# Differential attention on one core: head norm and exponentials later in each engine's order, weights scaled in one pass, mask by matmul, output projection in two parts

## The reference

```python
kv = rmsnorm(h, kv_norm_g) @ kv_w          # k1, k2: 64 wide, v: 128 wide, for each of 8 heads
qq = rmsnorm(h, b_norm_g) @ b_w_q          # q1, q2: 64 wide
k1, k2, q1, q2 = (apply_partial_rope(rmsnorm(.., g), cos, sin))   # norm over 64, rotation
...
def probs(qb, kk):
    s = einsum('bhqd,bhkd->bhqk', qb, kk) * scale
    return softmax(where(causal, s, -inf), axis=-1)
w = probs(q1b, k1f) - lam * probs(q2b, k2f)     # a block of 128 queries at a time
o = einsum('bhqk,bhkd->bhqd', w, v)
o = rmsnorm(o, b_subln_g) * (1.0 - lam_init)    # norm over a head's 128
h = h + merge_heads(o) @ b_w_o
h = h + squared_relu_mlp(h, ...)
```

## Time and profile before

| what | value |
|---|---|
| median of 3 runs | 3060.82 us (3059.88 to 3062.23) |
| profiled execution, own time | 3060.37 us |
| its span | 3058.6 us |
| TensorE matmul busy | 2711.6 us (89%) |
| DVE busy | 1170.4 us (38%) |
| ACT busy | 1036.7 us (34%) |
| GpSimd busy | 878.5 us (29%) |
| differential attention and its projection | about 2221 to 2682 us of the span |

### The profile page before, as it was taken

The page is one execution under the profiler, slowest core; times in us unless marked ns, Lnnn a source line. Parts: engine busy times, 40 slices in busy tenths (PEclk is TensorE's granted clock), DMA queues, the critical chain, the costliest instruction groups (busy, mean ns, idle before and its releaser), DMA issues.

```text
span 3058.6 us, 42262 instructions
## 1 busy us (share of the span) xinstructions
PE 2711.6 (89%) x16806; PEld 2200.1 (72%) x16806; DVE 1170.4 (38%) x2247; ACT 1036.7 (34%) x2154; POOL 878.5 (29%) x612
## 2 busy tenths in 40 slices
PE   4999898999989888888888789999987787799999
PEld 3887687787865555556777579999976665577777
DVE  4654556432241112112255751422555555212112
ACT  3434444522232112113234444233244544332331
POOL 0001454322320223100322126555410000355653
PEclk8989999999989999999899889999998887799999
DMA  3322011233327999993211012332311110123332
GB/s 105 84 57 55 15 35 35 77 97 89 101 96 295 426 426 426 426 425 141 77 45 51 23 49 83 97 90 86 88 52 39 42 28 8 56 83 97 97 92 67
DMA packets 320134, 364.16 MB, mean 119 GB/s; under 512 B 14128, under 2 KB 293680, under 8 KB 295360
## 3 DMA queue, kind: packets, MB, share of 16 engines
q1 hardware_dynamic: 319936, 361.42, 34.0%
HBM read 359.29 MB, written 2.10 MB: 118 GB/s over the span
## 4 chain that ended last, share of the span: by engine, by line
PE 67%; DVE 11%; DMA 8%; ACT 7%; POOL 4%; issue 4%; DVEq 0%; ACTq 0%; SPq 0%; POOLq 0%
DMA early<-in_w_up_e 7%; PE bank L1703 5%; PE bank L2160 5%; PE bank L443 5%; PE bank L445 5%; PE bank L444 5%; PE bank L2161 5%; PE bank L2162 5%; PE bank L2591 4%; PE bank L2592 4%; PE bank L2593 4%; POOL split L2133 2%; ACT split L2117 1%; PE bank L1001 1%; DVE split L2136 1%
## 5 line engine op out<-in xcount | busy, mean ns | idle before, releaser
L2133 POOL TENSOR_TENSOR split<-keep,split 128x1024 fp32r<-128x1024 f32 x152 | 369.6, 2436 | 357.7 <-ACT split L2113 357.7
L2160 PE MATMUL bank<-x_hi,split 128*128 128x264 f32 (+1 forms) x1280 | 401.5, 314 | 12.6 <-POOL split L2133 8.3
L2161 PE MATMUL bank<-x_lo,split 128*128 128x264 f32 (+1 forms) x1280 | 395.9, 309 | 0.0
L2162 PE MATMUL bank<-x_hi,split 128*128 128x264 f32 (+1 forms) x1280 | 394.8, 308 | 0.0
L1703 PE MATMUL bank<-early 128*64 128x256 f32 x2048 | 236.0, 385 | 48.3 <-DMA early<-in_w_up_e 19.8
L2160 PEld LDWEIGHTS bank<-x_hi,split 128*128 128x128 f32 x1280 | 245.0, 191 | 40.8 <-issue 26.2
L1703 PEld LDWEIGHTS bank<-early 128*64 128x64 f32 x2048 | 170.7, 138 | 126.7 <-issue 52.9
L2161 PEld LDWEIGHTS bank<-x_lo,split 128*128 128x128 f32 x1280 | 245.3, 192 | 10.2
L2162 PEld LDWEIGHTS bank<-x_hi,split 128*128 128x128 f32 x1280 | 244.3, 191 | 10.9
L2113 ACT ACTIVATE split<-keep 128x1024 fp32r<-128x1024 f32 x168 | 175.4, 1050 | 224.3 <-PE bank L2593 210.8
L443 PE MATMUL bank<-x_hi,w_split 128*128 128x512 f32 x416 | 169.8, 408 | 15.7 <-DVE w_split L431 15.7
(11 more groups left out here) (458 smaller groups left out, 6227.5 us busy)
## 6 DMA issues: line engine op xcount, KB each, us to landing
early<-in_w_gate_e SPq DMA_DIRECT2D x64, 1024.0 KB, 11.0
early<-in_w_up_e SPq DMA_DIRECT2D x64, 1024.0 KB, 11.2
early<-in_w_down_e SPq DMA_DIRECT2D x64, 1024.0 KB, 10.6
early<-in_w_in SPq DMA_DIRECT2D x66, 512.0 KB, 3.7
keep<-in_mlp_w_in SPq DMA_DIRECT2D x64, 512.0 KB, 3.9
keep<-in_mlp_w_out SPq DMA_DIRECT2D x64, 512.0 KB, 4.0
keep<-in_a_w_qkv SPq DMA_DIRECT2D x24, 512.0 KB, 3.6
early<-in_w_ssd_out SPq DMA_DIRECT2D x16, 512.0 KB, 4.0
```

The source lines that it names most:

```text
L2133: e.tensor_tensor(lo, x, whole(hi), ALU.subtract).then_inc(*u.free(sig_, "lo", n))
L2160: e.matmul(o, hi[:, k, :], XH2[:, k, n0:n1], start=k == 0, stop=False, skip_group_check=True)
L2161: e.matmul(o, hi[:, k, :], XL2[:, k, n0:n1], start=False, stop=False, skip_group_check=True)
L2162: m = e.matmul(o, lo[:, k, :], XH2[:, k, n0:n1], start=False, stop=k == 7, skip_group_check=True)
```

## The change

- **Weights with a gain.** A new helper `split_gain` on DVE multiplies the loaded tile by its gain in place, in one tensor_tensor; `split_hi` and `split_lo` then treat all tiles alike, with one instruction each. `split_gain` runs up to one tile ahead of the copy. In the attention `split_hi` and `split_lo` go one tile further ahead for j = 0 to 3.
- **Order inside a step.** The pieces of a step are now h3, h1, c2, c1, c0, lin, (first), (second), h0, h2, ce. `c0` ends with the maximum; the exponentials and the mixing are the new piece `ce`, behind the step's `lin`. The head norm is cut into h0 (square, lag 4), h1 (sum, lag 6), h2 (root, lag 6) and h3 (scaling and split, lag 7), and uses the head's own q and k buffers in place of a score buffer.
- **Projection step on DVE.** Before: low split, V, (sine, sum) of both halves, scaling, PSUM copy. After: V, sine of both halves, scaling, gain, sum of both halves, low split, PSUM copy. GpSimd's cosine product waits for the rotation matmul, not for DVE's sine.
- **Mask.** Two matmuls of an fp32r identity with an fp32r mask add it to the scores' last 128 columns in PSUM. ACT makes both operands in `normb_act`; TensorE waits for them at the start of the attention. The maximum is now written negated.
- **Scores of the last query block** are issued half by half, the two softmaxes in turn.
- **Output projection in two parts.** Its weights are now 8 tiles of 4 heads by 256 columns, split by ACT and DVE. For each of the 8 output tiles the first four heads (12 matmuls) are done in the attention's late steps (`first`) and added to the residual; `second` does heads 4 to 6 for four output tiles in steps 34 and 37; `outb_pe` does the rest.

```diff
-        plan += [(wbo, 0, 8, c, 128, None) for c in COLS8]
+        plan += [(wbo, k0, 4, 256 * c, 256, None) for k0 in (0, 4) for c in range(4)]
...
+        def split_gain(e, upto):
...
+                if gain is not None:
+                    e.wait_ge(*KW.of(n).landed())
+                    x = split_parts(n)[0]
+                    e.tensor_tensor(x, x, bc(gain[:, k0:k0 + nk], nc_), ALU.mult).then_inc(*S.dve.up("gain", n))
...
-                    for k in range(nk):
-                        e.scalar_tensor_tensor(out=lo[:, k, :], in0=x[:, k, :], scalar=gain[:, k0 + k:k0 + k + 1],
-                                               in1=whole(hi[:, k, :]), op0=ALU.mult, op1=ALU.subtract).then_inc(*u.free(sig_, "lo", n))
+                e.tensor_tensor(lo, x, whole(hi), ALU.subtract).then_inc(*u.free(sig_, "lo", n))
...
+            for y, x in ((IDENT2, C["ident"]), (NEG2, C["amask"][:, 128:256])):
+                e.activation(y, x, ACT.Copy).then_inc(*LM.act.up("mask"))
...
-        for step in range(37):
-            ATTB += [(f, step - lag) for f, lag in (("c4", 5), ("c3", 4), ("c2", 3), ("c1", 2), ("c0", 0)) if 0 <= step - lag < 32]
+        PARTS = (24, 25, 26, 28, 29, 30, 32, 33)
+        for step in range(39):
...
+            ATTB += units(("h3", 7), ("h1", 6), ("c2", 3), ("c1", 2), ("c0", 0))
             p, n = step // 8, step % 8
             if p < 3:
                 ATTB += [("lin", (p + 1, j)) for j in ([n] if n < 7 else [7, 8])]
+            if step in PARTS:
+                ATTB.append(("first", PARTS.index(step)))
+            if step in (34, 37):
+                ATTB.append(("second", range(4, 6) if step == 34 else range(6, 7)))
+            ATTB += units(("h0", 4), ("h2", 6), ("ce", 0))
...
         def attb_pe(e):
+            e.wait_ge(*LM.act.to("mask"))
...
+                    for a in range(2):
+                        e.matmul(XR.of("score", i, a, h).ap[:, kl - 128 - k0:kl - k0], IDENT2, NEG2, start=False, stop=True,
+                                 skip_group_check=True).then_inc(*DA2.pe.up("score", i, a, h))
...
-                    split_hi(e, attb_weights(p, j) + (2 if j < 4 else 3))
+                    split_hi(e, attb_weights(p, j) + 3)
...
-                    e.tensor_tensor(dg, dg, bmid(C["amask"][:, 128:256], 2), ALU.add).then_inc(*DA2.dve.up())
-                    e.wait_ge(*DA2.dve.now())
-                    e.tensor_reduce(out=v[:, 0:2], in_=xv[:, :, 0:kl], op=ALU.max, axis=AX.X).then_inc(*DA2.dve.up())
-                    e.wait_ge(*DA2.dve.now())
-                    e.tensor_scalar(v[:, 2:4], v[:, 0:2], -1.0, None, ALU.mult).then_inc(*DA2.dve.up("max", i))
+                    e.tensor_reduce(out=v[:, 2:4], in_=xv[:, :, 0:kl], op=ALU.max, axis=AX.X, negate=True).then_inc(*DA2.dve.up("max", i))
+                if what == "first":
+                    split_lo(e, AT_WBO + i // 2 + 3, True)
+                    b, r = BR.of("oa", "b", i), R[:, i, 16:T2]
+                    e.wait_ge(*OB_.pe.to("first", i))
+                    e.tensor_tensor(r, r, b.ap[:, :], ALU.add).then_inc(*b.free(OB_.dve, "first", i))
...
-                        e.wait_ge(*PD.dve.to("sin", i[0], i[1] - 2, h))
+                        e.wait_ge(*PD.pe.to("rot", i[0], i[1] - 2, h))
```

156 lines of the change are left out of this document (106 added, 50 removed).

## The result

| what | before | changed |
|---|---|---|
| median in the first comparison | 3060.62 us (3059.88 to 3062.23) | 3014.61 us (3010.11 to 3016.47) |
| profiled execution, its span | 3060.37, 3058.6 us | 3014.8, 3013.0 us |
| mean granted clock | 0.941 | 0.952 |

The ratio is 0.9846, 95% interval 0.9834 to 0.9857: the kernel is faster by 46 us (44 to 51 by the interval). The forecast was 2986 us (2945 to 3030), 74 us less than before. The direction and the wide range hold. The narrow range of the forecast itself, 2966 to 3006 us, is missed by 9 us: over a third of the forecast gain isn't there.

A forecast was written before the change was run, and what follows sets the result against it. The prediction saw no engine full: TensorE idled on waits for V's weight split and the head norm's square, and paid again in clock. 3060.4 + 9 (start) - 45 (passes) - 38 (tail) = 2986 us, own range 2966 to 3006, wide 2945 to 3030.

The forecast's parts named there:

- Tail: Last units alone plus output projection: 78 us instead of 116, -38 us (-28 to -44), with projection matmuls beside late units.
- Start: First nine projection steps: new waits for the mask and behind the roots, shorter V wait, clock loss; +9 us (2 to 14).
- Lookahead and V's wait: V's second weight tile split a step ahead: TensorE's wait 3 us or less in a pass, near 5 at the start.
- Single pass over the weights: One DVE product, ACT copy and DVE subtraction per tile: product 1.23 us; ACT relieved of about 7 us in a pass.
- A pass: Eight units with nine projection steps: 62 + 1.2 + 9.5 + 6 = 79 us instead of 94, -15 each, -45 for three.
- All 37.1 us of waiting go: Moved head norm: TensorE's waits for its square vanish, except for the last head.
- Work in a pass: TensorE's work at full clock: 62 us from busy time by clock, plus 1.2 us for mask matmuls.
- MLP 1: Last MLP, after the output projection: first tile split in time, its 363 us don't move.
- Lock: Rival, 8%: GpSimd's cosine products each hold up a DVE operation on the path, 18 us in all; 3004 us.
- DVE's loop: Rival, 16%: DVE's loop sets the pass, new waits full, pass 89 us, start +14, tail -30; 3028 us.
- TensorE stays fed: Rival, 15%: DVE runs ahead and no bank is late; pass 67 us, start +6, tail -42; 2945 us.
- Slower: Rival, 4%: DVE, PSUM copy and next linear close a loop in all eight steps, 13.5 us each; pass 108, total 3086 us.

The follow-up runs named there:

- tail_late: Changed kernel with the output projection's `first` and `second` matmuls issued behind all attention units instead of between the late ones; 3034.83 us, ratio 0.9909 to before.
- norm_old: Changed kernel with the head norm's square, sum and root together again ahead of the product with V, as before the change; 3024.52 us, ratio 0.9882.
- mask_late: Changed kernel with TensorE's wait for the mask's copies moved to the first unit's mask matmul; 3002.98 us, ratio 0.9807 to before.
- weights_first: Changed kernel with DVE's gain product and low-split subtraction at the beginning of its projection step; 2978.36 us, ratio 0.9728 to before.
- gain_old: Changed kernel with weights made by 8 or 4 scaled ACT copies and fused DVE operations again, new lookahead kept; 3007.96 us, ratio 0.9830.
- lookahead_old: weights_first with high and low weight parts split one tile less ahead for k, k, q, q, as before the change; 3011.44 us, ratio 0.9838.
- square_late: Changed kernel with ACT's square of a projection step one step later, behind the next unit's score copy; 2985.83 us, ratio 0.9746 to before.
- root_early: Changed kernel with the head norm's root on ACT right behind the unit's scores instead of at the step's end; 2996.54 us, ratio 0.9781.
- four_moves: Changed kernel with the moves of root_early, square_late, weights_first and mask_late all together; 2943.94 us, ratio 0.9615 to before.
- moves_gain_old: four_moves with weights made by 8 or 4 scaled ACT copies and fused DVE operations again; 2949.56 us, ratio 0.9641 to before.

## Why the prediction was right or wrong, point by point

- **Tail: right, the exact hit partly by luck.** 78 us (-38) forecast, 77.7 us (-38.3) measured on the marks of the earlier trace rows. The hand schedule came to 75 us and was 2.7 us short; the 3 us added for the clock weren't lost (it is 1.00), and the two errors cancel. By tail_late 17 us come from the matmuls beside the units, by norm_old 11 from the head norm; the wait of 6.6 us ahead of the projection is gone as well. The last 4 us have no run.
- **Start: right in its parts.** +6 us by the windows, forecast +9 (2 to 14). The wait for the mask is 5.42 us (5.7 forecast), the split behind the roots 4.63 us (4), V's wait 4.98 us (5.5). mask_late takes away the first, weights_first the other two. Too large was the clock: 5.4 + 4.6 - 5 leaves about 1 us for it, where the forecast had 4.
- **Lookahead and V's wait: right.** "3 us or less in a pass" is 2.7, 2.7 and 1.6 us.
- **Single pass over the weights: right that it costs little.** The product over a broadcast gain has a mean of 1218 ns, the estimate was 1.23 us. gain_old and lookahead_old (the latter on weights_first) confirm that the lookahead counted and not the number of instructions.
- **A pass: wrong, -6.5 us instead of -15 (-7.1 like against like); this is the failed step.** The term "62 + 1.2 + 9.5 + 6 = 79" measured 87.5 (86.9). Its idle time is (262.5 - 219.6)/3 = 14.3 us, not 9.5, and of another kind. The prediction laid out DVE's queue only. It had the square waiting for DVE's PSUM copy, and the exponentials behind it, but asked only whether the *linears* would wait for a bank. It didn't go down ACT's own queue to see what else stands behind the square and which bank that frees. The three waits of linears, 2.0, 3.1 and 1.4 us, hardly exist: TensorE had been held earlier, by 5.97 us (two passes) and 6.7 us (all three), and finds DVE done afterwards. The passes' waits are the 23.1 us of scores and 11.9 us of the product with V, 7.0 us for V's split and 0.7 us: together 42.7 of the 42.9 us of idle time. square_late takes away the cause and root_early one of its two effects.
- **"All 37.1 us of waiting go": right in the letter only.** The sum no longer waits; but h2 now frees the sum's bank at the end of ACT's step, and the product with V waits for that. norm_old shows a move worth nothing within the passes. The prediction named this case ("only swaps one wait for another") inside a rival that it gave another cause.
- **Work in a pass: 3 us too small.** 62 us came from busy time by granted clock. At nearly full clock, in four_moves, the same product is 205.13 x 0.97 / 3 = 66.3 us, where the forecast had 63.2. Three things make up these 3.1 us. The later marks put 14 more matmuls into the passes, 0.6 us for each pass. The two mask matmuls of a unit take 0.28 us and not 0.14:

```profile
2554.68 0.44 PE L2824 MATMUL bank<-mask 128*128 128x128 f32 x2
2554.96 0.45 PE L2759 MATMUL bank<-b_hi,split 128*128 128x512 f32 x1
```

  That is 2.2 us in a pass instead of 1.2; the forecast took 0.07 us out of its bounds of 0.06 to 0.14, and 0.14 was right. The other 1.5 us are the product itself: a stretch's mean clock also counts the idle time, in which it was partly low (before, from 2500.80 to 2504.70 us, TensorE does nothing and the granted clock is 0.50), so the product falls short where there are waits. The start shows the same: 50.75 x 0.89 = 45 us before, 47.74 x 1.00 = 48 us in four_moves, and only 0.5 us of that are the first unit's scores. By these terms the pass's miss of 8.8 us is 4.8 us of idle time, 3.1 of work and 0.9 of clock.
- **MLP 1: missed, +6 us.** In its first 20 us 66 matmuls start instead of the 83 before, at a clock of 0.91 against 1.00. The waits of PE there name two that before has not:

```profile
PE bank L2218 <- POOL squares_n L2208: 1.6, 1, 1.6
PE bank L2164 <- DVE x_lo L2198: 0.7, 1, 0.7
```

  The 17 matmuls are 17 x 0.235 = 4 us, of which these waits are 2.3 and the lower clock the rest: in four_moves, with the same waits and a clock of 1.00 there, 73 matmuls start and MLP 1 takes 381.2 us. Both waits belong to the norm between projection and MLP, which the prediction didn't lay out. No run took them away, and the last 2 us are left without a place.
- **The rivals.** *Lock*: its 3004 us are nearest to the measured time, but its cause isn't seen. DVE is busy 149.46 us in the passes against 158.47, and its sum of sine and cosine, the neighbour of GpSimd's products, takes 463 ns against 433; 24 times 0.03 us is under 1 us, where the rival had 18. The exclusion that the Trainium skill (SBUF — State Buffer, "Who interferes with whom") states for such pairs may act here, but no row shows a loss of the rival's size from it. *DVE's loop*: its pass of 89 us is nearer to the measured 87.5 than the forecast's 79, and its remark that a moved norm may only swap waits came true. But its waits, of linears for DVE's copy, aren't there, its start and tail were too bad by 8 us each, and four_moves excludes that DVE's work sets the pass. *TensorE stays fed*: its mechanism wasn't in this kernel, but four_moves shows it can be had: 2944 us where the rival said 2945. That is luck, since the division is another (passes -66 instead of -79, start -14 instead of +6). *Slower*: a step is 10.9 us (87.5/8), far from 12.6.

## What to carry to other kernels

When a step is delayed on one engine, write down for each engine what stands *behind* the delayed instruction in its queue and which buffer that would free, not only who reads its result; here a square that nobody needed for a whole step held back banks of both groups, and its place cost 28 us of 262. An instruction without a wait belongs where its engine idles, ahead of those that wait (DVE's weight work), and one that waits long belongs as late as its reader allows. Take the work of a stretch from matmul counts at full clock rather than from busy time by mean clock.

## What was not expected

- A wait taken away gave back more than its length. root_early removed 12 us of waiting, put 3.4 us in at the next linears and won 17.5 us in the passes, at a clock of 0.92 instead of 0.88. After the wait of 6.71 us, the next linear's 48 matmuls began at 2417.65 with 0.53 us for the first and took until 2424.93, 7.3 us, where 48 of them take 5.90 us at full clock.
- Stages that no edit touches differ between the profiled executions: MLP 0 ends between 2217.7 us (moves_gain_old) and 2226.8 us (four_moves) of the span, 9 us apart. Part of it is there at the very beginning: the granted clock of the first 200 us is 0.94 in mask_late and moves_gain_old and 0.92 in the changed kernel and four_moves. Whether it belongs to the kernel or to the one execution that was profiled isn't shown; four_moves' profiled execution took 2950.38 us where the median is 2943.94. Differences of a few microseconds between two kernels are therefore read in the stage's own length, not in the total: of mask_late's 12 us only 6.7 are its own.
